# Neighbourhood attention by two heads at a time, in a fused two-block network

## The reference, cut to what matters

```python
q, k, v = jnp.split(a_lat @ w_qkv, 3, axis=-1)
qc, kc, vc = jnp.split(a_ctx @ w_qkv, 3, axis=-1)
q_grid = (_heads(q, NA_HEADS) * scale)          # scale = 64 ** -0.5 = 0.125
...
s_lat = einsum('bjqhd,bjkhd->bhjqk', q_blk, k_blk) + bias
s_lat = jnp.where(mask, s_lat, -jnp.inf)
s_ctx = einsum('bjqhd,bkhd->bhjqk', q_blk, kc)
p = jax.nn.softmax(jnp.concatenate([s_lat, s_ctx], axis=-1), axis=-1)
o = (einsum('bhjqk,bjkhd->bjqhd', p[..., :n_lat], v_blk)
     + einsum('bhjqk,bkhd->bjqhd', p[..., n_lat:], vc))
```

## Time and profile before

| | |
|---|---|
| median of 3 runs | 3778.58 us |
| profiled execution | 3774.8 us |
| its span | 3773.0 us |
| TensorE busy | 92% of the span |
| VectorE, ScalarE busy | 67%, 50% |
| granted TensorE clock, mean | 0.951 |
| the attention stage in the span | 1426.1 to 1517.8 us |

### The profile page before, as it was taken

One profiled execution on the slowest core, in us unless ns is written; L12 is line 12 of the kernel. 1 busy time (PEld: TensorE's weight loads), 2 busy tenths in 40 slices (PEclk: granted clock), 3 DMA queues, 4 the chain that ended last, 5 costly groups with the idle time before them and its releaser, 6 DMA issues.

```text
span 3773.0 us, 70951 instructions
## 1 busy us (share of the span) xinstructions
PE 3460.4 (92%) x27016; PEld 3020.6 (80%) x27016; DVE 2537.6 (67%) x3378; ACT 1889.9 (50%) x2511; POOL 149.7 (4%) x161
## 2 busy tenths in 40 slices
PE   6966696879999999899999999999999999999899
PEld 4854383768989885788888888888899899998898
DVE  2456657555555627689999999999656655557555
ACT  3222222123344424478888888888544644444643
POOL 0068000000000000000000000000000000000000
PEclk8977797989999999899999999999999999999999
DMA  5222303003545530289999999999454355554354
GB/s 199 92 93 95 135 3 142 7 19 124 182 154 181 183 117 12 100 327 362 363 359 364 362 360 363 361 362 362 157 181 159 108 166 181 164 181 149 96 189 156
DMA packets 199350, 723.28 MB, mean 192 GB/s; under 512 B 21888, under 2 KB 25472, under 8 KB 198784
## 3 DMA queue, kind: packets, MB, share of 16 engines
q1 hardware_dynamic: 198576, 714.01, 53.7%
q0 software_dynamic: 592, 6.69, 0.4%
HBM read 719.57 MB, written 1.05 MB: 191 GB/s over the span
## 4 chain that ended last, share of the span: by engine, by line
PE 83%; DVE 6%; POOL 4%; ACT 3%; DMA 2%; issue 1%; SPq 1%; DVEq 0%; ACTq 0%; POOLq 0%
PE ps L305 23%; PE ps L306 23%; PE ps L307 23%; PE ps L657 1%; DMA ada_late<-wada 1%; PE ps L1432 1%; PE ps L525 1%; POOL ptmp L1207 1%; PE ps L1429 1%; POOL ptmp L1210 1%; PE ps L1699 1%; POOL ptmp L1208 1%; PE ps L1716 1%; PE ps L1423 1%; PE ps L2032 1%
## 5 line engine op out<-in xcount | busy, mean ns | idle before, releaser
L268 DVE TENSOR_TENSOR w_lo<-w_raw,w_hi 128x1024 fp32r<-128x1024 f32 x529 | 647.2, 1225 | 751.9 <-ACT w_hi L264 748.9
L264 ACT ACTIVATE w_hi<-w_raw 128x1024 fp32r<-128x1024 f32 x529 | 558.7, 1058 | 800.4 <-PE ps L307 741.4
L305 PE MATMUL ps<-a_hi,w_hi 128*128 128x256 f32 (+1 forms) x3000 | 895.8, 299 | 66.6 <-DVE a_lo L552 24.5
L2117 DVE TENSOR_TENSOR mlo<-mraw,mhi 128x1024 fp32r<-128x1024 f32 x726 | 877.1, 1224 | 91.9 <-ACT mhi L2113 62.8
L306 PE MATMUL ps<-a_lo,w_hi 128*128 128x256 f32 (+1 forms) x3000 | 897.1, 299 | 0.0
L307 PE MATMUL ps<-a_hi,w_lo 128*128 128x256 f32 (+1 forms) x3000 | 894.2, 298 | 0.0
L2113 ACT ACTIVATE mhi<-mraw 128x1024 fp32r<-128x1024 f32 x726 | 770.5, 1062 | 180.3 <-PE ps L307 149.1
L305 PEld LDWEIGHTS ps<-a_hi,w_hi 128*128 128x128 f32 x3000 | 578.3, 193 | 92.5 <-issue 51.4
L306 PEld LDWEIGHTS ps<-a_lo,w_hi 128*128 128x128 f32 x3000 | 572.3, 191 | 16.1 <-issue 0.5
L307 PEld LDWEIGHTS ps<-a_hi,w_lo 128*128 128x128 f32 x3000 | 572.5, 191 | 15.8
L305 PE MATMUL ps<-mhi,x_hi 128*128 128x512 f32 x968 | 395.5, 409 | 1.9 <-DVE mlo L2117 1.9
(11 more groups left out here) (495 smaller groups left out, 4642.4 us busy)
## 6 DMA issues: line engine op xcount, KB each, us to landing
mraw<-wexp SPq DMA_DIRECT2D x726, 512.0 KB, 5.3
w_raw<-wstream SPq DMA_DIRECT2D x529, 512.0 KB, 3.3
ada_late<-wada SPq DMA_DIRECT2D x80, 512.0 KB, 4.8
ada_raw<-wada SPq DMA_DIRECT2D x16, 512.0 KB, 9.1
bia<-bias POOLq DMA_DIRECT2D x1, 4096.0 KB, 14.2
con<-consts SPq DMA_DIRECT2D x1, 1824.0 KB, 16.1
conb<-constsb POOLq DMA_DIRECT2D x1, 1224.0 KB, 7.6
hT<-ctxT SPq DMA_DIRECT2D x1, 1024.0 KB, 12.4
```

What stands on the lines that cost most here:

```text
L264: nc.scalar.activation(whi[:, slot, :], raw[:, slot, :], ACT.Copy).then_inc(hi_ready.sem, 1)
L268: nc.vector.tensor_tensor(wlo[:, slot, :], raw[:, slot, :], whi[:, slot, :].bitcast(F32), ALU.subtract).then_inc(lo_ready.sem, 1)
L305: nc.tensor.matmul(out, lhs[0], rhs[0], start=start, stop=False, skip_group_check=skip)
L2117: nc.vector.tensor_tensor(mlo[:, slot, :], mraw[:, rslot, :], mhi[:, slot, :].bitcast(F32), ALU.subtract).then_inc(lo_ready.sem, 1)
```

## The change

The unit becomes a pair p of heads (2m and 2m+1, `m = p // 2`) and one query tile (`p % 2`), 16 in all. `scores(p)` issues two products, head after head, one in each row half, into two neighbouring banks (0 and 1, or 6 and 7). The scale goes into ScalarE's copy of q. VectorE adds the bias to the latent halves of both banks in place in PSUM, takes both maxima from PSUM in one instruction, and ScalarE's exponentials read PSUM. A bank is free again when the exponentials are done, where it was free after VectorE had read it. Eight transposes fill banks 2 and 3 together, one copy of 1024 per partition takes both out, and the transposes wait for the copy of the pair before. The value products alternate between the column halves. Scores are issued one pair ahead.

```diff
-            for n, dst, src in runs:
+            for n, dst, src, scale in runs:
...
+                    nc.scalar.activation(dst(t - first), src(5 + slot), ACT.Copy, scale=scale
+                                         ).then_inc(act_evac.sem, 1)
...
-                (8, lambda t: flat1(qT[:, one(t), :]), lambda b: ps[:, b, 0:SEG]),
+                (8, lambda t: flat1(qT[:, one(t), :]), lambda b: ps[:, b, 0:SEG], 0.125),
...
+        def sbanks(p):
+            return 6 * (p % 2)
+
+        def score_keys(p):
+            return p // 2, p % 2, slice(p % 2 * P, p % 2 * P + P)
...
+            def scores(p):
+                m, _, q = score_keys(p)
+                if p >= 2:
+                    pe.wait_ge(*S("exp_done").next("pe", 2))
+                for e in range(2):
+                    last = nc.tensor.matmul(ps[:, sbanks(p) + e, :], qT[hp(e), m, q], kT[hp(e), m, :],
+                                            start=True, stop=True)
+                last.then_inc(*S("sc_ps").one)
+
+            def transposes(p):
                 pe.wait_ge(*S("p_ready").next("pe"))
+                if p >= 1:
+                    pe.wait_ge(*S("pT_sb").next("pe_banks"))
+                for e in range(2):
+                    for kt_ in range(4):
+                        last = nc.tensor.transpose(ps[:, 2 + e, kt_ * P:(kt_ + 1) * P],
+                                                   pP[:, p % 2, e, kt_ * P:(kt_ + 1) * P], ident[:])
+                last.then_inc(*S("pT_ps").one)
+
+            def values(p):
+                m, _, q = score_keys(p)
+                pe.wait_ge(*S("pT_sb").next("pe"))
+                if p % 2 == 0 and p >= 4:
+                    pe.wait_ge(*S("at_sb").next("pe"))
                 for kt_ in range(4):
...
+                    for e in range(2):
+                        h = 2 * m + e
+                        last = nc.tensor.matmul(ps[hp(e), 4 + m % 2, q], vT[:, kt_, h * 64:(h + 1) * 64],
+                                                pT[:, p % PT_BUFS, e, kt_ * P:(kt_ + 1) * P],
+                                                start=(kt_ == 0), stop=(kt_ == 3))
                 last.then_inc(*S("at_ps").one)
             scores(0)
-            scores(1)
-            for u in range(2 * NH):
-                if u + 2 < 2 * NH:
-                    scores(u + 2)
-                transposes(u)
-                if u >= 1:
-                    values(u - 1)
-            values(2 * NH - 1)
...
+            for p in range(NPAIR):
+                if p + 1 < NPAIR:
+                    scores(p + 1)
+                transposes(p)
+                if p >= 1:
+                    values(p - 1)
+            values(NPAIR - 1)
...
-                link(nc.vector.tensor_scalar(sS[:, u % 2, 0:SEG], ps[:, sbank(u), 0:SEG], 0.125, None, ALU.mult))
-                nc.vector.scalar_tensor_tensor(sS[:, u % 2, SEG:T2], ps[:, sbank(u), SEG:T2], 0.125,
-                                               bia[:, h, qt * 256:(qt + 1) * 256], ALU.mult, ALU.add
-                                               ).then_inc(*S("sc_read").one)
...
+                link(nc.vector.tensor_tensor(ps[:, b:b + 2, SEG:T2], ps[:, b:b + 2, SEG:T2],
+                                             bia[:, 2 * m:2 * m + 2, qt * 256:(qt + 1) * 256], ALU.add))
+                link(nc.vector.tensor_reduce(mxv[:, c], ps[:, b:b + 2, :], AX.X, ALU.max))
+                nc.vector.tensor_scalar(nmx[:, c], mxv[:, c], -1.0, None, ALU.mult).then_inc(*S("nmx").one)
+
+            def norm(p):
+                dve.wait_ge(*S("exp_done").next("dve", 2))
+                link(nc.vector.reciprocal(rc_[:, 2 * p:2 * p + 2], sm[:, 2 * p:2 * p + 2]))
+                for e in range(2):
+                    u = 2 * p + e
+                    ins = nc.vector.tensor_scalar(pP[:, p % 2, e, :], pP[:, p % 2, e, :], rc_[:, u:u + 1], None, ALU.mult)
+                    if e == 0:
+                        link(ins)
+                ins.then_inc(*S("p_ready").one)
...
             soft(0)
-            for u in range(2 * NH):
-                if u + 1 < 2 * NH:
-                    soft(u + 1)
-                norm(u)
...
+            for p in range(NPAIR):
+                if p + 1 < NPAIR:
+                    soft(p + 1)
+                norm(p)
...
+            def ex(p):
                 act.wait_ge(*S("nmx").next("act"))
...
+                for e in range(2):
+                    u = 2 * p + e
+                    nc.scalar.activation(pP[:, p % 2, e, :], ps[:, sbanks(p) + e, :], ACT.Exp, bias=nmx[:, u:u + 1],
+                                         accum_out=sm[:, u:u + 1]).then_inc(*S("exp_done").one)
+
+            def cp(p):
                 act.wait_ge(*S("pT_ps").next("act"))
...
+                if p >= PT_BUFS:
                     act.wait_ge(*S("at_ps").next("act"))
...
+                nc.scalar.activation(pT[:, p % PT_BUFS, :, :], ps[:, 2:4, :], ACT.Copy).then_inc(*S("pT_sb").one)
```

More of the change, by code:

```diff
@@ L1621, in build @@
         NH = 16
-        qT, kT, vT, bia, sS, pP, pT, mxv, nmx, sm, rc_, oA, _r = lay(arena + 8192, [
+        PT_BUFS = 2
+        qT, kT, vT, bia, pP, pT, mxv, nmx, sm, rc_, oA, _r = lay(arena + 8192, [
             ("qT", [P, 8, SEG]), ("kT", [P, 8, T2]), ("vT", [P, 4, D]), ("bia", [P, NH, 512]),
-            ("sS", [P, 2, 512]), ("pP", [P, 2, 512]), ("pT", [P, 2, 512]), ("mxv", [P, 32]), ("nmx", [P, 32]),
+            ("pP", [P, 2, 2, 512]), ("pT", [P, PT_BUFS, 2, 512]), ("mxv", [P, 32]), ("nmx", [P, 32]),
             ("sm", [P, 32]), ("rc_", [P, 32]), ("oA", [P, 8, SEG])])
@@ L1671, in act_copies, with after @@
             first = 0
-            for n, dst, src in runs:
-                def after(t, slot, dst=dst, src=src, first=first):
+            for n, dst, src, scale in runs:
+                def after(t, slot, dst=dst, src=src, scale=scale, first=first):
                     act.wait_ge(tile_used.sem, used(base, t))
-                    nc.scalar.activation(dst(t - first), src(5 + slot), ACT.Copy).then_inc(act_evac.sem, 1)
+                    nc.scalar.activation(dst(t - first), src(5 + slot), ACT.Copy, scale=scale
+                                         ).then_inc(act_evac.sem, 1)
                 run_tiles(act, "act", base, n, t0=first, after=after, ahead=0 if first else 1)
@@ L1683, in act_qkv @@
             act_copies(act, BASE["qkv"], [
-                (8, lambda t: flat1(qT[:, one(t), :]), lambda b: ps[:, b, 0:SEG]),
-                (8, lambda t: flat1(kT[:, one(t), :]), lambda b: ps[:, b, :])])
+                (8, lambda t: flat1(qT[:, one(t), :]), lambda b: ps[:, b, 0:SEG], 0.125),
+                (8, lambda t: flat1(kT[:, one(t), :]), lambda b: ps[:, b, :], 1.0)])
             act_values(act, BASE["qkv"] + 16)
-        def sbank(u):
-            return (0, 1, 6)[u % 3]
+        NPAIR = NH
@@ L1702, in transposes @@
-            def transposes(u):
-                pe.wait_ge(*S("p_ready").next("pe"))
-                for kt_ in range(4):
[L1705 to L1718, removed]
+            def scores(p):
[6 more added lines that the diff above has]
+                last.then_inc(*S("sc_ps").one)
@@ L1719, in values @@
                 last.then_inc(*S("at_ps").one)
             scores(0)
-            scores(1)
-            for u in range(2 * NH):
-                if u + 2 < 2 * NH:
-                    scores(u + 2)
-                transposes(u)
-                if u >= 1:
-                    values(u - 1)
-            values(2 * NH - 1)
-            pe.wait_ge(*S("sc_read").next("pe", 3))
+            for p in range(NPAIR):
[4 more added lines that the diff above has]
+                    values(p - 1)
@@ L1730, in pe_attn @@
+            values(NPAIR - 1)
+            pe.wait_ge(*S("exp_done").next("pe", 4))
             pe.wait_ge(*S("at_sb").next("pe", 2))
@@ L1733, in dve_attn, with soft @@
             dve.wait_ge(S("bias").sem, 16)
-            def soft(u):
-                h, qt = u // 2, u % 2
+            def soft(p):
+                m, qt, _ = score_keys(p)
+                b, c = sbanks(p), slice(2 * p, 2 * p + 2)
                 dve.wait_ge(*S("sc_ps").next("dve"))
-                link(nc.vector.tensor_scalar(sS[:, u % 2, 0:SEG], ps[:, sbank(u), 0:SEG], 0.125, None, ALU.mult))
-                nc.vector.scalar_tensor_tensor(sS[:, u % 2, SEG:T2], ps[:, sbank(u), SEG:T2], 0.125,
-                                               bia[:, h, qt * 256:(qt + 1) * 256], ALU.mult, ALU.add
-                                               ).then_inc(*S("sc_read").one)
[L1743 to L1752, removed]
+                link(nc.vector.tensor_tensor(ps[:, b:b + 2, SEG:T2], ps[:, b:b + 2, SEG:T2],
+                                             bia[:, 2 * m:2 * m + 2, qt * 256:(qt + 1) * 256], ALU.add))
@@ L1754, in out @@
             def out(m):
-                dve.wait_ge(*S("at_ps").next("dve", 4))
+                dve.wait_ge(*S("at_ps").next("dve", 2))
```

(27 more changed lines are left out.)

## The result

The changed kernel takes 3824.22 us (median of 4 runs, 3819.84 to 3824.97) against 3779.36 for the one before in the same rounds: +44.9 us, a ratio of 1.011 with a 95% interval of 1.0098 to 1.0122: slower by 1.1%, clear of noise. Forecast were 3818 and +39.6.

A forecast was written before the change was run, and what follows sets the result against it. TensorE and VectorE alternate in the attention stage: start 6.5, 14 rounds of 8.4 (117.6) less 1.6, end 8.1 and 0.7, total 131.3 against 91.7; 3778.6+39.6 = 3818 us, range 3787 to 3840.

The forecast's parts named there:

- The order: Attention stage: scores(p+2) queue behind transposes(p), so the round spans one pair, not two; 6.5 us at full clock against 5.32.
- TensorE's leg at full clock: TensorE's part of a pair's round: handover, eight transposes, values and scores, 0.05+1.02+1.02+1.17 = 3.26 us.
- The halves: Score products in two row halves, values in two column halves overlap fully; rival without overlap: about +61, 3840, chance 0.07.
- only in program order: Rival: score products overlap only as issued, three slots instead of two, 0.43 more per pair; +13, 3831, chance 0.06.
- VectorE's leg: Bias addition in PSUM, double maximum, negation to two norms: 0.725+1.255+1.27 = 3.25 us per pair, all exposed.
- The clock: TensorE's pauses lower its clock: work of 3.2 at 0.63 of full speed, 5.1 us, making the round 8.4.
- The ends for the clock: Rivals for the stage: all full clock 102.3 (+10.6, 3789, chance 0.06); all low 143.7 (+52, 3831, chance 0.07).
- VectorE's pace: Fast rival: scores(p+2) start before transposes(p), VectorE unbroken at 3.5 per pair; stage 60.3, -31, 3747; chance 0.06.
- Edits at nothing: Scale in ScalarE's q copy, exponentials from PSUM, copy of transposed banks: mostly covered; the copy shows only at the end.

The follow-up runs named there:

- experiment 1: The changed kernel with scores issued two pairs ahead instead of one: 3752.93 us, ratio 0.9928 to the kernel before; run again 3747.34 us; stage 59.9 and 60.6.
- experiment 3: The kernel before, by single heads, with scores issued one unit ahead instead of two: 3904.10 us, ratio 1.0331, stage 215.2.
- experiment 2: The changed kernel, order kept, with 12 useless identity products before every group of transposes: 3795.78 us, ratio 1.0041 to the kernel before, stage 106.0.
- experiment 4: The kernel of experiment 1 with both score products of a pair in one row half (odd heads' scores left out): 3770.76 us, ratio 0.9965, stage 81.9.
- experiment 7: The kernel of experiment 1 with both heads' value products in one column half, head after head: 3755.63 us, ratio 0.9946, stage 69.5.
- Experiment 6: The kernel of experiment 1 with the eight output copies moved from VectorE to ScalarE: 3749.61 us, ratio 0.9916 to the kernel before, stage 59.6.

## Why the prediction held

*The order, as the step from which all follows:* right, and shown by experiments 1 and 3, which moved only the lookahead, in either kernel: 134 to 60 with pairs, 92 to 215 without.

*TensorE's leg at full clock,* 3.26: measured 1.03+1.02+1.18+0.05 = 3.28 in experiment 2. *The halves* overlap fully, as rows 4 and 5 had it; experiments 4 and 7 price them at 0.85 and 0.87 a pair, the forecast figures. The rival "only in program order" falls with the start of the changed stage: weight loads four, two, two, and four products in 1.99, where that order would need an extra slot of 0.43. The Trainium skill, "TensorE: Matmul & The Clock Gate", Part 3, The mechanism, has matmuls start strictly in program order. The trace disagrees: two products run side by side in the first 0.2 us, and by experiment 4 the two instructions of one head don't, so they are the first ones of the two heads, ahead of the first head's second. That reading takes it that the compiled program keeps the source's order, which no row prints.

*VectorE's leg,* 3.25: measured 3.27. The addition in PSUM took 0.700 behind a wait and 0.69 without one (0.69 taken from the earlier trace rows), the double maximum 1.225 (1.22):

```profile
L1752 DVE TENSOR_REDUCE mxv<-ps 128x2 f32<-128x1024 f32 x16 | 19.6, 1225 | 0.6
...
L1750 DVE TENSOR_TENSOR ps<-ps,bia 128x512 f32<-128x512 f32 x16 | 11.2, 700 | 78.2 <-PE ps L1706 78.2
```

*The clock* was the largest term and the least certain: TensorE's part 5.1 of a round forecast, 5.3 measured in the 13 full rounds (1445.95 to 1557.93, 8.61 each, less 3.27 and 0.05). The stage came to 134.3 against 131.3: 2.8 more in these rounds, nearly all of it the clock; 0.5 in the first round, which has no values and took 1445.95-1438.60 = 7.35 where 6.8 were put; start and end together 0.3 less. The ends for the clock were rightly not taken: all high would be 102 (experiment 2, which forces it: 106), all low 144.

*VectorE's pace,* the fast rival, was wrong for this order. Its price, 60.3 and -31 for a stage in which scores(p+2) come before transposes(p), stands beside 59.9 and -27 to -33 when experiment 1 issued them so. That closeness is in part luck: the 15 rounds took 49.3 where 3.47 each make 52.1, and what follows the last addition 9.4 where the price has about 7. *Edits at nothing* held; the exponentials from PSUM took 0.683 against 0.722 from SBUF, unseen on the path.

The total's last 5 us of difference (44.9 to 39.6) are 3.0 in the stage and what lies outside it, for which the study has only the spread of parts that don't differ.

## What to carry to other kernels

When a change makes the unit of a software pipeline larger, count how many units the loop from one engine back to itself spans, before and after: the old loop of 5.2 us spanned two units and hid under 2.66 each, the new of 6.5 spanned one and hid nothing. Experiment 6 shows the same loop coming back as the bound once the engine that hid it gets faster. Where a buffer is free before the wait that stands in front of it in the queue, issue its producer ahead of that wait. And price pauses of TensorE twice, once as time and once as clock: here the second was two to three times the first (28.3 to 14.3, or an estimated 31.0 to 11.6).

## What the runs showed of the hardware

Useless products can pay: 192 of them in TensorE's pauses brought the granted clock from 0.70 to 1.00 and the stage from 134.3 to 106.0. But a TensorE that is busy in every record isn't always granted the high level: in experiment 4 it was busy 20.00 of 20 us from 1440 to 1460 at 0.50. VectorE's addition of 128x512 is as fast with its result in PSUM as in SBUF (0.69, or 0.700 behind a wait, against 0.691). Two float32 products of 512 columns in the two row halves take 1.13 together, in one half 1.98.
